# Moving twelve small loads to another queue and halving the first norm at the start of a two-block transformer kernel

## The reference, cut to what matters

```python
def rmsnorm(x, g):
    xf = x.astype(jnp.float32)
    y = xf * lax.rsqrt(jnp.mean(xf * xf, axis=-1, keepdims=True) + EPS)
    return (y * g.astype(jnp.float32)).astype(x.dtype)
...
    h = rmsnorm(x, g_mix[l])
    proj = jnp.einsum("bsd,de->bse", h, w_in[l])
    (q_s, k_s, v_s, q_d, k_d, v_d, q_i, k_i, w_i, q_m, gate_logits) = jnp.split(proj, split_points, axis=-1)
...
    m = rmsnorm(mem, g_mem[l])
    mkv = jnp.einsum("bmd,de->bme", m, w_mem_kv[l]).reshape(B, M, 2, N_MEM_HEADS, HEAD_DIM)
```

## Time and profile before

| | |
|---|---|
| median of 3 runs | 2773.07 us (2770.81 to 2773.09) |
| the profiled execution | 2767.88 us |
| its span | 2766.1 us |
| mean granted TensorE clock | 0.965 of full speed |
| TensorE busy | 2509.3 us, 91% of the span |
| DVE, ACT, POOL busy | 58%, 44%, 31% |

### The profile page before, as it was taken

The page is one execution under the profiler, slowest core; times in us unless marked ns, Lnnn a source line. Parts: engine busy times, 40 slices in busy tenths (PEclk is TensorE's granted clock), DMA queues, the critical chain, the costliest instruction groups (busy, mean ns, idle before and its releaser), DMA issues.

```text
span 2766.1 us, 32782 instructions
## 1 busy us (share of the span) xinstructions
PE 2509.3 (91%) x11852; PEld 2037.6 (74%) x11852; DVE 1592.0 (58%) x2780; ACT 1215.0 (44%) x2236; POOL 862.1 (31%) x756
## 2 busy tenths in 40 slices
PE   4997899997879799999999989987598999999997
PEld 3765778885668677777888867876486888877885
DVE  5357459875463687875545843335747444355675
ACT  6146357736212545444434443225415555543343
POOL 0222422221140255653243300004102656514142
PEclk9999999998999999999999989999898999999998
DMA  4102123334152267768755422222232444395344
GB/s 153 44 20 75 43 69 96 96 102 149 51 178 96 75 197 231 220 212 260 279 166 163 134 95 74 79 77 79 85 134 70 151 161 148 129 345 181 131 155 143
DMA packets 190128, 369.77 MB, mean 134 GB/s; under 512 B 13692, under 2 KB 58372, under 8 KB 189716
## 3 DMA queue, kind: packets, MB, share of 16 engines
q1 hardware_dynamic: 177620, 340.46, 37.5%
q10 hardware_dynamic: 8064, 14.68, 1.4%
q0 software_dynamic: 4288, 12.60, 1.4%
HBM read 266.95 MB, written 100.74 MB: 133 GB/s over the span
## 4 chain that ended last, share of the span: by engine, by line
PE 73%; DVE 12%; DMA 5%; ACT 5%; issue 4%; POOL 2%; SPq 0%; DVEq 0%; ACTq 0%; POOLq 0%
PE bank L2167 9%; PE bank L2168 9%; PE bank L2169 9%; PE bank L2536 7%; PE bank L2538 7%; PE bank L2537 7%; PE bank L2510 5%; PE bank L2512 5%; PE bank L2511 5%; DMA ada<-in_w_ada 3%; DVE ada_sum L1824 2%; PE bank L2344 1%; PE bank L2345 1%; PE bank L2346 1%; DVE w_lo L1414 1%
## 5 line engine op out<-in xcount | busy, mean ns | idle before, releaser
L2510 PE MATMUL bank<-hq_hi,wq_hi 128*128 128x512 f32 x896 | 354.8, 396 | 17.3 <-DVE hq_lo L1832 11.2
L2536 PE MATMUL bank<-ring_b_hi,ring_a_hi 128*128 128x512 f32 x896 | 351.3, 392 | 13.8 <-DVE xs L1877 8.4
L2512 PE MATMUL bank<-hq_hi,wq_lo 128*128 128x512 f32 x896 | 352.6, 394 | 0.0
L2511 PE MATMUL bank<-hq_lo,wq_hi 128*128 128x512 f32 x896 | 351.9, 393 | 0.0
L2537 PE MATMUL bank<-ring_b_lo,ring_a_hi 128*128 128x512 f32 x896 | 350.3, 391 | 0.0
L2538 PE MATMUL bank<-ring_b_hi,ring_a_lo 128*128 128x512 f32 x896 | 350.1, 391 | 0.0
L1919 DVE TENSOR_TENSOR ring_a_lo<-a_raw,ring_a_hi 128x1024 fp32r<-128x1024 f32 x112 | 146.3, 1306 | 233.4 <-ACT ring_a_hi L1242 233.2
L1242 ACT ACTIVATE ring_a_hi<-a_raw 128x1024 fp32r<-128x1024 f32 x112 | 118.7, 1060 | 341.2 <-PE bank L2538 320.7
L2510 PEld LDWEIGHTS bank<-hq_hi,wq_hi 128*128 128x128 f32 x896 | 170.4, 190 | 57.7 <-DVE hq_lo L1832 15.9
L1771 DVE TENSOR_TENSOR wq_lo<-unit_raw,wq_hi 128x512 fp32r<-128x512 f32 x160 | 159.2, 1001 | 87.3 <-ACT wq_hi L1108 85.2
L2536 PEld LDWEIGHTS bank<-ring_b_hi,ring_a_hi 128*128 128x128 f32 x896 | 169.0, 189 | 53.3 <-DVE xs L1877 7.4
(11 more groups left out here) (452 smaller groups left out, 5810.8 us busy)
## 6 DMA issues: line engine op xcount, KB each, us to landing
a_raw<-hidden_scratch SPq DMA_DIRECT2D x112, 512.0 KB, 3.3
hidden_scratch<-hidden SPq DMA_DIRECT2D x32, 1024.0 KB, 5.1
w_raw<-in_w_in SPq DMA_DIRECT2D x104, 256.0 KB, 2.9
ada<-in_w_ada SPq DMA_DIRECT2D x96, 256.0 KB, 3.0
hidden_scratch<-hidden SPq DMA_DIRECT2D x32, 768.0 KB, 4.7
unit_raw<-in_w_mlp_in SPq DMA_DIRECT2D x16, 1024.0 KB, 8.3
b_raw<-in_w_mlp_out SPq DMA_DIRECT2D x32, 512.0 KB, 4.6
unit_raw<-in_w_ff SPq DMA_DIRECT2D x16, 1024.0 KB, 5.3
```

The lines of the kernel that those rows point to most:

```text
L2510: mm(o, lh[:, q, :], rh[:, q, :], start=(fresh and q == 0), stop=False, skip_group_check=True)
L2511: mm(o, lh[:, q, :], rl[:, q, :], start=False, stop=False, skip_group_check=True)
L2512: l = mm(o, ll[:, q, :], rh[:, q, :], start=False, stop=(q == 3), skip_group_check=True)
L2536: mm(o, ra_hi[r][:, e, js], rb_hi[r][:, e, :], start=(fresh and v == 0 and e == 0), stop=False, skip_group_check=True)
```

## The change

Five things change, all in the opening. (1) The twelve small loads are issued by ACT, on its own DMA queue, as the first thing in its list; SP issued them between the second and the third `xin` load. (2) SP issues `memx`, the four `xin` loads and the first four pieces of `C_MEM` without anything between. (3) ACT takes the root of the memory rows directly after their two sums, then sums four `xin` tiles, takes their root, and does the other four tiles later. (4) DVE and TensorE follow: the first four tiles are normed and transposed, then the other four. (5) The eight pieces of `C_MEM` and of `C_Q` are split in two times four with transposed rows between, and TensorE transposes the second half of the input rows in pairs behind each of the four memory groups. One more root makes the later counts on `n_v` one higher.

```diff
@@ SyncE
             sp.dma_start(memx[:, :, :], mem_v).then_inc(mem_in, 16)
             for j in range(4):
-                sp.dma_start(xin[:, 2 * j:2 * j + 2, :], x_v[:, 2 * j:2 * j + 2, :]).then_inc(x_in[j], 16)
-                if j != 1:
-                    continue
-
-                for name, row, n in (("g_mix", c_gmix, 8), ("g_mem", c_gmem, 8), ("b_gate", c_bgate, 24),
...
-                    sp.dma_start(vrow[row:row + n, :], v.rearrange("(k p) -> k p", p=P)).then_inc(vec_in, 16)
-                sp.dma_start(posi[:, :], a["positions"][0].rearrange("(k p) -> k p", p=P)).then_inc(vec_in, 16)
-                sp.dma_start(sink_in[:, :], a["sinks"].broadcast_to([P, 8])).then_inc(vec_in, 16)
-            for c, pieces in enumerate(FIRST):
-                load_chunk(c, pieces)
+                x_load(j)
+            load_chunk(C_MEM, FIRST[0][0:NRAW])
+            load_chunk(C_MEM, FIRST[0], range(NRAW, 8))
+            for c, pieces in enumerate(FIRST[1:]):
+                load_chunk(c + 1, pieces)
@@ ScalarE
+            for name, row, n in (("g_mix", c_gmix, 8), ("g_mem", c_gmem, 8), ("b_gate", c_bgate, 24),
...
+                act.dma_start(vrow[row:row + n, :], v.rearrange("(k p) -> k p", p=P)).then_inc(vec_in, 16)
+            act.dma_start(posi[:, :], a["positions"][0].rearrange("(k p) -> k p", p=P)).then_inc(vec_in, 16)
+            act.dma_start(sink_in[:, :], a["sinks"].broadcast_to([P, 8])).then_inc(vec_in, 16)
...
             norm_sums(memx, range(2), 8, lambda j: (mem_in, 16) if j == 0 else None, 0)
-            norm_sums(xin, range(8), 0, lambda j: (x_in[j // 2], 16) if j % 2 == 0 else None, 2)
-            act.wait_ge(n_v, 1)
-            A_(rst[:, 0, 8:10], rst[:, 1, 8:10], ACT.Sqrt).then_inc(n_sq, 1)
-            act.wait_ge(n_v, 2)
-            A_(rst[:, 0, 0:8], rst[:, 1, 0:8], ACT.Sqrt).then_inc(n_sq, 1)
+            root(0, 8, 10)
+            x_sums(0, 4)
+            root(1, 0, 4)
             act.wait_ge(cols_ok, 1)
-            split_hi(C_MEM, 0, None)
             norm_hi(0, [(memT[0][:, k, :], c_gmem + k, MEM) for k in range(8)])
-            norm_hi(8, [(hT[h][0][:, k, :], c_gmix + k, 512) for h in range(2) for k in range(8)])
-
-            split_hi(C_Q, 1, None)
+            split_hi(C_MEM, 0, None, range(4))
+            norm_hi(8, [(hT[0][0][:, k, :], c_gmix + k, 512) for k in range(8)])
+            x_sums(4, 8)
+            root(2, 4, 8)
+            split_hi(C_MEM, 0, None, range(4, 8))
+            norm_hi(16, [(hT[1][0][:, k, :], c_gmix + k, 512) for k in range(4)])
+            split_hi(C_Q, 1, None, range(4))
+            norm_hi(20, [(hT[1][0][:, k, :], c_gmix + k, 512) for k in range(4, 8)])
+            split_hi(C_Q, 1, None, range(4, 8))
@@ TensorE
+            x_transposes(0, 0, 8)
             chunk_ready(C_MEM)
             pe.wait_ge(n_lo, 8)
             w = W[0]
             for j in range(2):
                 group(j, j, MEM, [((w[0][:, k, j * P:(j + 1) * P], w[1][:, k, j * P:(j + 1) * P]),
                                    (memT[0][:, k, :], memT[1][:, k, :])) for k in range(8)])
+                x_transposes(1, 2 * j, 2 * j + 2)
```

More of the change, by code:

```diff
@@ L404, in _, with load_chunk @@
         def _(sp):
-            def load_chunk(c, pieces):
-                for p, src in enumerate(pieces):
+            def load_chunk(c, pieces, which=None):
+                for p in which or range(len(pieces)):
+                    src = pieces[p]
                     if 8 * c + p >= NRAW:
@@ L915, in norm_hi @@
                     A_(dst, XB[(n0 + n) % 4][:, 0:w], ACT.Copy, scale=cols[:, gain:gain + 1]).then_inc(n_hi, 1)
[L917 to L922 removed]
+            for name, row, n in (("g_mix", c_gmix, 8), ("g_mem", c_gmem, 8), ("b_gate", c_bgate, 24),
+                                 ("g_mlp", c_gmlp, 8), ("g_mix_2", c_gmix2, 8), ("g_ffn_2", c_gffn2, 8),
+                                 ("g_head_2", c_ghead, 4), ("pool_scale_2", c_pool, 4), ("c_2", c_c, 8),
+                                 ("b_ada_2", c_ada, 48)):
+                v = a[name]
+                v = v[0] if v.shape[0] == 1 else v
+                act.dma_start(vrow[row:row + n, :], v.rearrange("(k p) -> k p", p=P)).then_inc(vec_in, 16)
@@ new lines, in _, with root, x_sums @@
+            act.dma_start(posi[:, :], a["positions"][0].rearrange("(k p) -> k p", p=P)).then_inc(vec_in, 16)
+            act.dma_start(sink_in[:, :], a["sinks"].broadcast_to([P, 8])).then_inc(vec_in, 16)
+            def root(k, lo, hi):
+                act.wait_ge(n_v, k + 1)
+                A_(rst[:, 0, lo:hi], rst[:, 1, lo:hi], ACT.Sqrt).then_inc(n_sq, 1)
+            def x_sums(t0, t1):
+                norm_sums(xin[:, t0:t1, :], range(t0, t1), t0,
+                          lambda j: (x_in[(t0 + j) // 2], 16) if (t0 + j) % 2 == 0 else None, 2 + t0)
@@ L1124, in roots @@
             def roots(j, h):
-                act.wait_ge(n_v, 3 + j)
+                act.wait_ge(n_v, 4 + j)
                 A_(rst[:, 0, 4 * h:4 * h + 4], rst[:, 1, 4 * h:4 * h + 4], ACT.Sqrt).then_inc(n_sq, 1)
@@ L1445, in _, with x_rows, x_lo @@
                 tsc(memx[:, j, :], memx[:, j, :], rst[:, 0, 8 + j:9 + j], None, ALU.mult).then_inc(n_xn, 1)
[L1446 to L1450, removed]
-            norm_lo(0, [(memT[0][:, k, :], memT[1][:, k, :], c_gmem + k, MEM) for k in range(8)])
-            norm_lo(8, [(hT[h][0][:, k, :], hT[h][1][:, k, :], c_gmix + k, 512) for h in range(2) for k in range(8)])
-            split_lo(C_Q, 1)
+            def x_rows(t0, t1, k):
+                dve.wait_ge(n_ss, 2 + t1)
+                norm_rstd(t0, t1, k)
+                for j in range(t0, t1):
+                    tsc(xin[:, j, :], xin[:, j, :], rst[:, 0, j:j + 1], None, ALU.mult).then_inc(n_xn, 1)
+            def x_lo(h, k0, k1):
+                norm_lo(8 + 8 * h + k0, [(hT[h][0][:, k, :], hT[h][1][:, k, :], c_gmix + k, 512) for k in range(k0, k1)])
+            x_rows(0, 4, 1)
+            norm_lo(0, [(memT[0][:, k, :], memT[1][:, k, :], c_gmem + k, MEM) for k in range(8)])
+            split_lo(C_MEM, 0, range(4))
+            x_lo(0, 0, 8)
+            x_rows(4, 8, 2)
+            split_lo(C_MEM, 0, range(4, 8))
+            x_lo(1, 0, 4)
+            split_lo(C_Q, 1, range(4))
+            x_lo(1, 4, 8)
+            split_lo(C_Q, 1, range(4, 8))
             dve.wait_ge(ifr_made, 1)
@@ L1760, in half_rstd @@
                 dve.wait_ge(n_ss, 10 + 4 * j + 4)
-                norm_rstd(4 * h, 4 * h + 4, 2 + j)
+                norm_rstd(4 * h, 4 * h + 4, 3 + j)
             def half_rows(h):
@@ L2197, in _, with x_transposes @@
                        lambda n: (n_xn, 2) if n == 0 else None)
-            transposes(8, [[xin[:, 4 * h + j, k * P:(k + 1) * P] for j in range(4)] for h in range(2) for k in range(8)],
-                       lambda n: (n_xn, 6 + n // 2) if n in (0, 8) else None)
+            def x_transposes(h, k0, k1):
+                transposes(8 + 8 * h + k0, [[xin[:, 4 * h + j, k * P:(k + 1) * P] for j in range(4)] for k in range(k0, k1)],
+                           lambda n: (n_xn, 6 + 4 * h) if n == 0 else None)
+            x_transposes(0, 0, 8)
             chunk_ready(C_MEM)
```

8 lines of the change are left out of this document (3 added, 5 removed).

## The result

| | before | after |
|---|---|---|
| median | 2773.01 us (2768.37 to 2779.38, 20 runs) | 2776.82 us (2772.85 to 2784.54, 20 runs) |
| ratio of the times, after to before | | 1.0019, 95% interval 1.0013 to 1.0025 |
| the profiled execution | 2767.88 us | 2784.54 us |
| its span | 2766.1 us | 2782.8 us |
| mean granted clock | 0.965 | 0.954 |

The change costs 5.3 us by the ratio (0.0019 x 2773; interval 3.6 to 6.9), 3.8 by the two medians. The kernel is slower, by just under the 0.2% that the prediction counted as no change. The time lies in the predicted range of 2773 to 2786; the point, 2783, is 6 us too high.

What follows compares the result with a forecast made beforehand. With TensorE busy 91% of the span, the start of `C_Q` was taken to set the time: 74.4 - 63.86 = +10.5 us, on 2773.07 giving 2783.6, stated as 2783, range 2773 to 2786.

Steps and rivals of the forecast that it cites:

- I take 19 us: Opening: the twelve small loads on ACT's queue land at 19 us, within bounds of 6.9 to 19.4.
- the 9 to 10 of one for one: Opening: if ACT's and SP's queues interleave one for one, the small loads land at about 9 to 10 us.
- One us late is one us: Opening, ACT's first root: from about 8.5 us on, each us the small loads are late makes everything a us late.
- The chain from landing to memory groups: Opening: serial norm, sums and splits on DVE and ACT run from the landing at 19.0 to the memory groups at 53.3.
- From the memory groups to `C_Q`: TensorE: half-rate start costs 2.1 us, the `C_Q` split is last, a stand-still of about 4 us; `C_Q` at 74.4.
- 0 to 1.7 us, I take none: Behind TensorE's stand-still ahead of `C_Q`: a lower clock may cost 0 to 1.7 us; none was counted.
- POOL's constants: Opening: POOL's constants wait for the late sums (46.5) and are read only in the position tables; no cost.
- With 13 us, halfway: Rival: small loads land halfway, at 13 us, `C_Q` starts at 67 to 68.6, time 2777; chance 0.15.
- The early case: Rival: small loads land at 9.5 us, `C_Q` at 65.1, +1.2 us and up to 1.7 more, 2775; chance 0.28.
- 0.8 us each: Rival: ACT's issues take 0.8 us each, squares start 5.6 us later; +3.5 us with early loads, nothing with late ones.
- The late case: Likeliest case: small loads land at 15 us or more, +7 to +11.5 us, 2780 to 2785; chance 0.5.

Runs made afterwards that it cites:

- a4: The kernel before with only the twelve small loads moved to ACT, at the head of its list: 2770.52 us, ratio 1.0002.
- b1: The changed kernel with the twelve small loads back on SP, between the second and third `xin` load: 2777.65 us, ratio 1.0023.
- c1: The changed kernel with the twelve small loads on SP behind the fourth `xin` load: 2782.69 us, ratio 1.0045.
- b2: The changed kernel with `C_Q` split in two fours, each ahead of four groups of the second half's transposed rows: 2772.33 us, ratio 1.0004.
- a1: The changed kernel with DVE norming the memory rows ahead of its wait for the small loads: 2772.18 us, ratio 1.0007.
- d1: The changed kernel with the edits of a1 and b2 together, nothing else: 2769.49 us, ratio 0.9990.
- a3: The changed kernel with 85 additional identity transposes on TensorE in the wait ahead of the memory groups: 2780.64 us, ratio 1.0037.

## Why the prediction was right in direction and 6 us too high

- **The step that failed: the landing of the small loads, "I take 19 us".** Measured 12.95. It lay between the bounds of 6.9 and 19.4; the choice of the upper one went by the row of 14.1 us, a transfer of POOL's queue at another place in the program, taken as nearest because SP's queue was full there too. Issued by ACT the loads landed at 12.95 and 12.81 (a4), issued by SP in line behind two `xin` loads at 13.16, 13.19 and 13.21, behind four at 18.71. So ACT's queue was served in between, at neither end. The profile after shows how: from 8 to 10 us ACT's queue (q10) finished 130 packets beside 186 of SP's (q1), and its last one fell between 12.5 and 13.

```profile
q1 hardware_dynamic: 186, 0.76, 95.7%
q10 hardware_dynamic: 130, 0.03, 7.6%
```

So it was served beside SP's from early on, and not after it. The estimate from the Trainium skill (page "DMA: Bandwidth & Descriptors", section "Queues, rings and completion order"), about 18 us by one turn for each of SP's large shares, was too late, and the 9 to 10 of one for one too early. The ratio of packets in the earlier trace rows was no measure either: it tells what both queues finished, not how long the last small load waits, and 2.7 to 1 neither shows turns packet by packet nor rules them out.
- **"One us late is one us".** Held: `C_Q` moves 5.7 us for 5.5 of landing from b1 to c1.
- **The chain from landing to memory groups.** 34.3 us predicted (19.0 to 53.3), measured 33.05 in the changed kernel and in c1 alike. It included 1.0 us that nobody had counted, POOL's hold on DVE, and was still too long by 1.2. Up to the first `xin` multiply 8.0 us passed instead of 8.6. And the chain let ACT's eight copies follow 32 transposes of 0.246 us that begin only behind the last `memT_lo`, 8.0 us; the first 16 ran from 25.91, ahead of its end at 27.13, the others at 2.63 us, and ACT was through at 33.74, 6.6 us behind it.
- **From the memory groups to `C_Q`.** 21.1 predicted, 21.5 measured; the low clock at their start cost 2.3 for 2.1 (1.7 to 3.1 in the other runs). That the split of `C_Q` would be last, with TensorE standing still for about 4 us, was right (4.24), and b2 shows that the order on ACT and DVE is its cause.
- **"0 to 1.7 us, I take none".** It came, 1.7 us, in the changed kernel and in a1, and not behind the 1.78 us of b2. It belonged in the sum.
- **"POOL's constants" at nothing.** They were put behind the sums and costed by who reads them. Their cost was who runs beside them: 1.0 us of DVE. It isn't shown that this moves the time.
- **The rivals.** "With 13 us, halfway, `C_Q` starts at 67 to 68.6: 2777" is what happened, 67.52 and 2776.8, and it was given 0.15. The early case (9.5 us) didn't come; ACT's issues took 5.1 us for the 4.5 said, not 0.8 us each. The late case was the likeliest by one row only; c1, which makes it, costs 12.5 us (8.6 to 16.4), with the said 10.5 inside its interval.

Summed again with the landing at 12.95: 2783.6 - 6.05, less 1.2 of the chain, plus 0.4 and 1.7, is 2778.4. By the ratio 2773.0 + 5.3 = 2778.3 was measured, by the medians 2776.8. These terms were read from the changed kernel itself, so the sum shows where the difference lies and is no second forecast. The time fell inside the stated 2773 to 2786 because that range was drawn through the other cases; the likeliest case's own, 2780 to 2785, missed it.

## What to carry to other kernels

An instruction that waits for another engine holds everything behind it in its own list: before an early step is moved up, ask what the other engine must have done by then, and take unrelated waits (here for twelve tiny loads) out of that engine's way. Moving work forward at one place pays only as far as the next step that needs both engines; here 6.3 us at the memory groups turned into a loss at the next weights, and only with their split moved ahead and the wait for the small loads gone did `C_Q` start earlier than before (d1). And where one unmeasured duration decides between rivals that are 6 us apart, the prediction's point is no better than the row chosen for it: a row of the same engine and the same stretch is worth more than the one that looks alike.

## What the runs showed of the hardware

- Twelve loads of 2 to 24 KB on ACT's queue, issued from 0.75 to 5.82 us beside 6 MB on SP's, landed hardly earlier (12.81 to 13.08 in the five kernels where DVE waits for them) than on SP's own queue between the second and third of four loads of 1 MB (13.16 to 13.21).
- 32 one-column writes of POOL (1.12 us together) held a DVE instruction on 4 columns for 1.17 us instead of 0.17. The Trainium skill, page "SBUF — State Buffer", section "SBUF: two separate sides", says that the two engines share one pair of ports as an exclusive lock held for a whole instruction, where VectorE's is in a two-port performance mode, or has two inputs in SBUF against a GpSimd instruction that reads SBUF. The rows agree that DVE was blocked; no row shows in which mode its instruction was. They show more, that it got no turn between POOL's 32.
- Waits of TensorE of 4.2 us ahead of `C_Q` were followed by 3.4 us at the lower level of the clock (0.66 over 5 us), and those of 1.8 us by none (1.00); after 3.72 us (a3) the clock fell too, though only 1.2 us after the matmuls had begun. The price of a wait isn't fixed: behind waits of 13.0 us it was 4.6 us at the lower level in one kernel (0.71 over 8 us, changed) and 6.2 in another (0.61, c1), and behind the waits of about 4 us for POOL's rotations 3.2 us (0.80, b2) or 5.8 (0.64, changed).
- The granted clock of these profiles was no measure until it changed for the first time. In the kernel before it reads 1.00 from 39.8 to 44, yet single transposes are half as long again there as a little later. Groups by line of TensorE before, 39.7 to 41.6 and then 46 to 49 us (busy us, mean ns of one, idle time before):

```profile
L2188 PE MATMUL bank<-ident,memx 128*128 128x128 f32 x8 | 2.0, 424 | 13.3 <-DVE memT_lo L1431 13.3
...
L2188 PE MATMUL bank<-ident,xin 128*128 128x128 f32 x20 | 3.3, 287 | 0.2 <-DVE hT_lo L1431 0.2
```

The prediction's lower level from 39.78 to about 44 was read from such lengths, and they bear it out; its clock column would not have shown it.
